# One sum of weight quarters moved from an adding transfer to an addition on GpSimd, in a one-core transformer step on Trainium2

## The reference

```
h  = modulate(rmsnorm(x, g_ffn), shift2, scale2)
x  = x + gate2 * ((silu(h @ w_gate) * (h @ w_up)) @ w_down)
```

## Time and profile before

| | us |
|---|---|
| median of 3 runs | 889.58 (888.97 to 889.75) |
| the profiled execution, its own time | 889.07 |
| its span, first to last instruction | 887.2 |
| PE busy | 875.1 (99%) |
| DVE busy | 707.3 (80%) |
| ACT busy | 467.4 (53%) |
| POOL busy | 122.3 (14%) |

### The profile page before, as it was taken

How to read it: one execution, slowest core, us unless ns; L and a number is a source line. 1 busy time by engine, 2 the same in 40 slices (tenths; PEclk the granted TensorE clock), 3 DMA queues, 4 the chain that set the end, 5 groups by cost and what they waited for, 6 DMA issues and landing times. The chain is left out here.

```text
span 887.2 us, 16538 instructions
## 1 busy us (share of the span) xinstructions
PE 875.1 (99%) x6227; PEld 832.4 (94%) x6227; DVE 707.3 (80%) x1331; ACT 467.4 (53%) x973; POOL 122.3 (14%) x155
## 2 busy tenths in 40 slices
PE   7999999999999999999999999999999999999998
PEld 5788888898989999999999999999999999999997
DVE  5567898899788499774777879997777898777887
ACT  6563444777777533432246645555544555545553
POOL 0000000010000000000000033313423322333221
PEclk9999999999999999999999999999999999999999
DMA  9964343541543220238307289868999886898867
GB/s 367 368 219 171 129 146 120 165 128 52 169 152 107 72 72 1 85 107 325 126 24 238 65 186 205 178 168 204 196 201 194 177 189 167 199 210 189 182 151 147
DMA packets 51663, 145.32 MB, mean 164 GB/s; under 512 B 6000, under 2 KB 12416, under 8 KB 50176
## 3 DMA queue, kind: packets, MB, share of 16 engines
q1 hardware_dynamic: 32000, 102.38, 35.0%
q0 software_dynamic: 18864, 41.11, 24.0%
q10 hardware_dynamic: 720, 0.77, 0.2%
HBM read 121.68 MB, written 12.20 MB: 151 GB/s over the span
## 5 line engine op out<-in xcount | busy, mean ns | idle before, releaser
L1320 ACT ACTIVATE w_hi<-stage 128x512 fp32r<-128x512 f32 (+1 forms) x186 | 105.7, 608 | 93.2 <-DMA stage<-stage 48.0
L2013 DVE TENSOR_TENSOR w_lo<-stage,w_hi 128x512 fp32r<-128x512 f32 (+1 forms) x186 | 117.7, 667 | 20.4 <-ACT w_hi L1320 20.0
L2628 PE MATMUL ps<-m_hi,w_hi 128*128 128x320 f32 x304 | 93.9, 309 | 0.0
L2628 PE MATMUL ps<-m_lo,w_hi 128*128 128x320 f32 x304 | 93.9, 309 | 0.0
L2628 PE MATMUL ps<-m_hi,w_lo 128*128 128x320 f32 x304 | 93.9, 309 | 0.0
L1415 DVE TENSOR_TENSOR w_lo<-stage,w_hi 128x1024 fp32r<-128x1024 f32 x47 | 57.2, 1222 | 35.9 <-ACT w_hi L887 35.5
L2628 PE MATMUL ps<-h_hi,w_hi 128*128 128x320 f32 x272 | 84.1, 309 | 0.8 <-DVE w_lo L2013 0.8
L2628 PE MATMUL ps<-h_hi,w_lo 128*128 128x320 f32 x272 | 84.0, 309 | 0.0
L2628 PE MATMUL ps<-h_lo,w_hi 128*128 128x320 f32 x272 | 84.0, 309 | 0.0
L2628 PE MATMUL ps<-y_hi,w_hi 128*128 128x320 f32 x264 | 81.7, 309 | 0.0
L2628 PE MATMUL ps<-y_hi,w_lo 128*128 128x320 f32 x264 | 81.6, 309 | 0.0
(11 more groups left out here) (317 smaller groups left out, 2437.0 us busy)
## 6 DMA issues: line engine op xcount, KB each, us to landing
stage<-w_main SPq DMA_DIRECT2D x118, 512.0 KB, 4.2
x<-w_ada SPq DMA_DIRECT2D x21, 512.0 KB, 4.5
stage<-stage POOLq DMA_DIRECT2D x38, 256.0 KB, 4.7
qk<-w_ada SPq DMA_DIRECT2D x7, 1024.0 KB, 13.8
scr<-w_main POOLq DMA_DIRECT2D x28, 256.0 KB, 6.2
y_t<-scr POOLq DMA_DIRECT2D x22, 320.0 KB, 6.7
s_second<-w_main POOLq DMA_DIRECT2D x26, 256.0 KB, 6.1
stage<-w_main POOLq DMA_DIRECT2D x19, 256.0 KB, 6.4
```

The lines of the kernel that those rows point to most:

```text
L1320: act.activation(w_hi[:, slot, at:at + job_half(j) * P], left_stage(op, j), ACT.Copy).then_inc(left_hi[op], 1)
L2013: dve.tensor_tensor(w_lo[:, slot, w], left_stage(op, j), w_hi[:, slot, w].bitcast(F32), ALU.subtract).then_inc(left_lo[op], 1)
L2628: ins = pe.matmul(ps[:, BANK_OF[op], 0:TH], wt[:, slot, w], right(op, part, j, k), start=k == 0 and n == 0, stop=k == half - 1 and n == 2)
```

## The change

The 20 additions that make S4 in the jobs behind up jobs are no longer DMAs that add `stage` to `stage`. Each is now an instruction of GpSimd, a `tensor_tensor` addition of two `stage` places into the first of them. It stands in the same place of POOL's program, behind the same two waits. Its semaphore `s4_sum` counts 1 for each sum, where a DMA counted 16, and `sum_made` is changed to match. Nothing else is changed.

```diff
             if sums_by_vector(j):
                 return {"S1": s1_own, "S2": s2_own, "S4": s4_own}[op], N_SEVEN + n
-            return {"S1": s1_sum, "S2": s2_sum, "S4": s4_sum}[op], 16 * n
+            return {"S1": (s1_sum, 16 * n), "S2": (s2_sum, 16 * n), "S4": (s4_sum, n)}[op]
...
                 pool.wait_ge(*sum_made("S2", j))
                 pool.wait_ge(left_lo["A12"], nth(j))
-                pool.dma_start(left_stage("S4", j), left_stage("S2", j), accum_op=ALU.add).then_inc(s4_sum, 16)
+                nc.gpsimd.tensor_tensor(left_stage("S4", j), left_stage("A12", j), left_stage("S2", j), ALU.add).then_inc(s4_sum, 1)
```

## The result

The changed kernel takes 892.34 us (median of 10 runs, 889.83 to 894.36), the kernel before 889.30 us beside it (10 runs, 888.42 to 890.41). The ratio is 1.0032, with a 95% interval of 1.0024 to 1.0040: slower, by 3.0 us. Two later comparisons of the same two kernels gave less, 1.0010 (0.9998 to 1.0022) and 1.0008 (0.9998 to 1.0018), 0.7 to 1.0 us; by themselves those two could not be told from no change. The size is therefore not settled to better than 0.7 to 3.0 us; no comparison shows a gain.

A forecast was written before the change was run, and what follows sets the result against it. PE, busy 99%, was taken to bound the kernel. Removing its 0.92 us stall, against 1.9 us of new stall from a library load, gave net +1.0: 889.07 to 890.1, plus 0.5 for the median, 890.6 us; range 888.4 to 896.8.

The forecast's parts named there:

- its line of 0.2%: Whole kernel: about 0.2% (1.8 us) is what a measurement can tell from no change.
- the sign of being wrong altogether: PE's job list: waits later than job 3, or matmuls slower than every 0.15 us, would refute the forecast.
- Removing the transfer wins at most 0.92 us: PE's stall at S4 of job 1, the only one in the job list, would go: -0.92 us.
- S4 is early by 2.9 us in each: Jobs after job 1: the addition makes S4 2.9 us sooner than the transfer, so POOL's queue catches up.
- The library load, X = 5.7 us, net +1.0 us: POOL before its first addition: code load of 5.7 us delays job 1; PE stalls 1.9 us instead of 0.92.
- Rival 1: POOL's library is resident or loads in under 1.9 us: -0.92 us, 888.7 us; chance 0.22.
- its chain: POOL's queue: late first addition delays S1, S3 and S2 of job 1 (S1 by 4.3 us), stalling PE at S4.
- The addition takes 1.04 us, DVE cost 0: Each GpSimd addition takes 1.04 us (bounds 0.52 to 1.73); holding up DVE costs 0, at most 20.8 us.
- Rival 3: GpSimd and DVE block each other at first down jobs 5, 17, 27: +3.1 us, 892.7 us; chance 0.08.
- ACT's 48.0 us of waits much reduced: ACT's 20 waits for adding transfers inside `stage`, 48.0 us before, would shrink much; a sign the forecast is right.

The follow-up runs named there:

- the kernel swapped and behind `w_lo` of S2: Changed kernel with S1 and first S3 term of job 1 issued before the first addition; later additions wait for `w_lo` of S2: 889.03 us, 0.9993 to before.
- the kernel that uses it early: Changed kernel plus a one-column GpSimd addition some 300 us before the job list, so the library loads there: 890.31 us, 1.0013 to before.
- the addition behind `w_lo` of S2: Changed kernel in which each addition also waits for `w_lo` of S2 of its own job: 891.38 us, 1.0021 to before.

## Why the prediction was right and wrong

**The outcome** lies in the range (888.4 to 896.8), on the side to which 0.45 was given; the median was put at 890.6 us, and 892.3 us came (890.6 in both later comparisons). By its line of 0.2% the first comparison is slower and the later two are no change. That the later medians meet the forecast is luck: its +1.0 us was the price of a load that cost nothing. The way there was wrong in its main term, and what the prediction itself named as the sign of being wrong altogether, waits of PE later than job 3, is there at jobs 5 and 17.

*Removing the transfer wins at most 0.92 us*: right as a ceiling, never reached. In the first trace of the changed kernel 0.44 us were still lost at that place, in the other two nothing; and in each trace without that stall job 5 is longer by 0.5 us or more, also where DVE's turn is 12.18 us. In the trace of before, DVE gains on PE while PE stands still at job 1 (it comes to line 2084 1.7 us into job 2, against 3.0 us in the kernel swapped and behind `w_lo` of S2), and that lead lasts to job 5; without the stall it is missing. That *S4 is early by 2.9 us in each* job was wrong as well: `w_lo` of S4 stands behind that of A11 on DVE, so it is DVE's place that decides, and in jobs 2 to 5 it was ready later than before, not earlier.

*The library load, X = 5.7 us, net +1.0 us*: wrong. No time of it can be seen: its row lies in a wait in the changed kernel and is one of 4 ns in the kernel that uses it early. Rival 1's condition (X under 1.9 us) was what happened, but not its time, since its sum took for granted that nothing else costs. The Trainium skill's figure of about 6 us for the first call to a freshly loaded kernel (GPSIMD Engine Reference, "Instruction dispatch") has no match here: the first call started 0.07 us after the load's row and took 0.30 us. What was right in that step is its chain. A late first addition moves S1, S3 and S2 of job 1 and ends as a stall at S4 of job 1; the addition behind `w_lo` of S2 showed it at 1.2 us.

*The addition takes 1.04 us, DVE cost 0*: the addition takes 1.29 us alone, inside the bounds of 0.52 to 1.73, but it does stand in DVE's way, 0.2 to 0.54 us in each of the tight jobs. The step that failed is the sentence "so an up job leaves DVE some 2.5 us. If each addition of GpSimd held DVE up for its whole length, 1.04 us, that fits." The stretch of the earlier trace rows on which it rests, 650 to 700 us, holds jobs 11 to 14 (and the first 2 us of job 15), in which DVE keeps PE's turn of 12.32 us with room to wait. Jobs 2 to 5 and 15 to 17 are of the other kind: DVE's turn there is 12.18 to 12.19 us of work and short waits for ACT (0.20 and 0.28 us), and leaves 0.13 us. One window with up jobs stood for all up jobs.

*Rival 3*, blocking in the first down jobs, had the right mechanism and 0.08 of the chance. Its price of 3.1 us came out near the first result by the wrong count: the blocking is paid in the jobs ahead, and is collected at the first down job, where PE needs the newest tile.

*ACT's 48.0 us of waits much reduced*: wrong, 50.0 us. 19 of the 20 transfers awaited, 46.6 us, were those of S2. POOL's wait for its S4 (59.0 us on the S2 landing) said the same in the trace of before, and was not read.

Still open: why the first comparison gave 3.0 us and the others 0.7 to 1.0. The trace of the first has 1.6 us of its excess ahead of the job list, where the kernels are the same; whether that falls by chance into one comparison's median was not shown.

## What to carry to other kernels

Ask of an engine that is to take a new neighbour how its slack is spread over the kinds of jobs, not what it is over a stretch: here DVE was idle for 2.4 us of a job of one kind, and in the other kind its turn was only 0.13 us shorter than PE's. Replacing a transfer that nothing awaits last has nothing to win, and the instruction put in its place can hold up the engine that feeds PE; if it must be, place it where that engine reads one SBUF operand, as in the kernels with the wait for `w_lo` of S2. A wait attributed to a tile by name should be checked for which of two transfers of that name it is, before it is counted as a gain.

## What the runs showed of the hardware that was not expected

- The GpSimd library load had no time of its own that a trace shows. Its row is 4 ns long in the kernel that uses the library early, with a one-column addition of 0.30 us right behind it; in the others it is 0.38 to 1.09 us long and ends 0.06 us after GpSimd's issue ahead of it.
- An addition on GpSimd of 512 float32 columns took 1.29 us, 2.5 ns for a column, where a copy takes 1.0 ns; beside DVE instructions that read two SBUF operands it took up to 2.13 us.
- The blocking goes both ways: GpSimd's addition grew by 0.84 us behind a DVE instruction under way and two that followed without a gap, and a DVE instruction of 0.48 us grew to 1.48 us behind it. The later one waits for the whole rest of the earlier, less 0.13 to 0.14 us, where DVE is the later.
- In the same traces no DVE instruction with one operand in PSUM is longer beside a GpSimd addition, and none with two SBUF operands across a GpSimd fill.
